# Mixers' output projection: four results side by side per input block, and high halves of its weights made on ScalarE

## The chip, the cores and the metric

The kernel runs on one core of a Trainium2 chip. The metric is the device time of one execution in microseconds (us), and smaller is better. TensorE is called PE in the rows (PEld is its weight load), VectorE DVE, ScalarE ACT, GpSimd POOL and SyncE SP.

## What is computed

The reference runs two blocks of a model over 256 tokens of 1024 channels, everything in float32. The first block has two layers. Each layer adds to the running state `h`, in this order: half of a gated feed-forward network, a "mixer", an attention to a memory of 256 rows, and half of a second feed-forward network. The change is in the mixer alone:

```python
p = u @ w_mix_in[l]
p_conv, p_hg, p_rw = jnp.split(p, (CONV_PROJ, CONV_PROJ + HG_PROJ), axis=-1)
y = jnp.concatenate([short_conv_mixer(p_conv, ...), hgrn2_mixer(p_hg, ...), rwkv7_mixer(p_rw, ...)], axis=-1)
h = h + y @ w_mix_out[l]
h = h + memory_cross_attention(rmsnorm(h, xattn_norm[l]), rmsnorm(mem, mem_norm[l]), ...)
```

`rwkv7_mixer` ends with a group norm over each head (mean and variance over 64 channels), a gain and an offset per channel, a bonus term and a gate; that gives the last 384 of the 1024 channels of `y`. `w_mix_out` is 1024 by 1024. The second block (attention over a context, a mixture of experts) follows and is not touched.

## The kernel before, in words

**Numbers in two halves.** A float32 product at the accuracy wanted is made from three products of a faster format: each operand is split into a high half (a cast, "hi") and a low half (the original minus the high half, "lo"), and `mm3` issues hi·hi, hi·lo and lo·hi into one PSUM bank. One block of 128 by 128 weights against 256 tokens is thus three matmuls (line 368, in `mm`).

**The weights come as a stream.** `Stream` (called `W`) holds all weights in the order of use, cut into chunks of 32 blocks (128 partitions by 4096 columns, 2 MB). SyncE loads chunk after chunk into three slots (L2103), and waits before each until TensorE has released the chunk that lay there. `split(c)` makes the two halves of chunk `c`, both on VectorE: a cast (L130) and a subtraction (L131). `blocks` hands out blocks in order. At the first block of chunk `c` it also queues `split(c + 1)`, so a chunk is split one chunk ahead; `prepare` queues the first split by hand. `toks` are the points of VectorE's queue that a matmul on the chunk waits for; each stands for eight blocks where a chunk was split in pieces.

**The queues.** Every engine takes its instructions in the order in which the program queued them, which is the order in which the Python code runs. On VectorE, ScalarE and GpSimd each instruction also waits for the one before it (`Queue`, chain true). There is no planner: an instruction that waits holds up all that are queued behind it on its engine. `barrier()` gives tokens for all that has been queued so far.

**PSUM.** `Banks` hands out the eight PSUM banks in turn; a matmul into a bank waits until the bank's last reader is done. During the mixer only banks 0 to 4 are in turn; before the output projection the turn is widened to all eight (`B.banks = psb`).

**The end of a mixer.** The order of the code, and so of the queues, is this. At the end of `rwkv` (call c the chunk with the first half of `w_mix_out`): the group norm's reductions on VectorE (L1135, L1139), a square root on ScalarE (L416 through `power`), the scaling by it on VectorE, and six transposes on TensorE (L397) into two banks, which are the last two of the five in turn. Then `W.prepare` queues `split(c)`. After it, for each of three groups of 128 channels, come four VectorE instructions (L405, L400: gain and offset, bonus, gate). Back in `mixer`: `Halves.make` splits `Y(5)` to `Y(7)` on VectorE (L388 the cast, L400 the subtraction); those of `Y(0)` to `Y(4)` were made before. `memory_squares` has GpSimd load the memory rows (L60, 1 MB), and queues on ScalarE eight squares of them (L416), which wait for that load. Then `linear` makes the eight results of the projection (m = 0 to 7), each from eight blocks (k = 0 to 7, one per 128 channels of `y`): 192 matmuls, two chunks, c and c + 1. For each result `evac2` adds it to `X(m)` (VectorE, L400) and calls `nxt.add`: the halves of the next norm's input on VectorE (L404, L408) and a square on ScalarE (L416). These halves are the operand of the next product, the attention's query (`xattn_wq`), whose first result needs all eight. Behind its first result stands `norms`, 32 matmul rows on TensorE for two root mean squares, and the chain on VectorE that hangs on them.

The order on ScalarE's queue around the projection is: the square root of the group norm, the eight squares of the memory rows, then one square for each result. On VectorE it is: `split(c)`, the twelve of the group norm's end, the halves of Y(5) to Y(7), `split(c + 1)`, the evacuations of m = 0 to 3 (three instructions each), `split(c + 2)`, the evacuations of m = 4 to 7, `split(c + 3)`.

Of the kernel before, what the change touches and what calls it, by code (L numbers as in the profile page):

```python
# [7 lines left out]
F32 = mybir.dt.float32  # L8
U32 = mybir.dt.uint32
F32R = mybir.dt.float32r  # L10
ALU = mybir.AluOpType
# [5 lines left out]
NHI = 2  # L17
D = 1024
KT = 8
# [89 lines left out]
class Stream:  # L109
# [3 lines left out]
    def __init__(self, ring, ring_r, hiring_r, sems, pe, dve, idle):  # L113
        self.ring, self.ring_r, self.hiring_r, self.pe, self.dve, self.idle = ring, ring_r, hiring_r, pe, dve, idle
        self.arrivals = [Arrival(s) for s in sems]
        self.specs, self.released, self.breaks, self.ahead, self.plain = [], {}, {}, {}, False

    def arrived(self, c):
        return (self.arrivals[c % NSLOT], 16 * (c // NSLOT + 1))

    def split(self, c, *after):

        n = CH * 128
        raw = self.ring[:, n * (c % NSLOT):n * (c % NSLOT) + n]
        lo = self.ring_r[:, n * (c % NSLOT):n * (c % NSLOT) + n]
        hi = self.hiring_r[:, n * (c % NHI):n * (c % NHI) + n]
        toks = []
        for a, b in ((0, 1024), (1024, 2048), (2048, 4096)) if c == 0 else ((0, 4096),):
            h, r, w = hi[:, a:b], raw[:, a:b], lo[:, a:b]
            self.dve(lambda e, h=h, r=r: e.tensor_copy(h, r), self.arrived(c), self.released.get(c - NHI), after)  # L130
            toks.append(self.dve(lambda e, h=h, r=r, w=w: e.tensor_tensor(w, r, h.bitcast(F32), ALU.subtract)))  # L131
        self.ahead[c] = (toks, len(self.dve.ops))

    def cancel(self, c):
# [138 lines left out]
def build(nc, x_t, mem_t, ctx_t, params, consts, na_bias, wexp, xd, yd, out, stop):  # L273
    es = ExitStack()
    with es:
# [36 lines left out]
        DVE = Queue("dve", True)  # L312
        ACTQ = Queue("act", True)
# [43 lines left out]
        def barrier():  # L357

            toks = [(q, q.n) for q in (DVE, ACTQ, POOL) if q.n]
            if PE.ops:  # L360
                toks.append(PE.mark())
            return toks
# [7 lines left out]
        def mm3(ps, a, b, start, stop, *after, inc=False):  # L370

            (ah, al), (bh, bl) = a, b
            mm(ps, ah, bh, start, False, after)
            mm(ps, ah, bl, False, False)
            return mm(ps, al, bh, False, stop, inc=inc)

        def as_r(ap):
            return arena_r[:, ap.offset:ap.offset + ap.shape[1]]
# [20 lines left out]
        def tt(q, out_, a, b, op, *after, **kw):  # L399
            return q(lambda e: e.tensor_tensor(out_, a, b, op), *after, **kw)  # L400
# [17 lines left out]
        def cp(q, out_, a, *after, **kw):  # L418
            if q is ACTQ:
                return q(lambda e: e.copy(out_, a), *after, **kw)  # L420
            return q(lambda e: e.tensor_copy(out_, a), *after, **kw)  # L421

        B = Banks(psb)

        def linear(key, r0, c0, nm, xs, evac, *after, kt=KT, n=256, between=None):

            toks = []
            for m in range(nm):
                ps, w = B.take()
                for k in range(kt):  # L430
                    wb, a = W.blocks(key, r0 + 128 * k, c0 + 128 * m)
                    t = mm3(ps[:, 0:n], wb, xs.at(k, 0, n), k == 0, k == kt - 1, w, a, after, xs.tok[k], inc=k == kt - 1)
                if m == 0 and between is not None:
                    between()
                tok = evac(m, ps, t)
                B.leave(ps, tok)
                toks.append(tok)
            return toks
# [179 lines left out]
        def mixer(l, pre, nxt):  # L618
            uh = pre.h
            Pr = Reg(8192, 29 * 256)  # L620
            P = lambda j, n=1: Pr.v(256 * j, 256 * n)
            Yr = Reg(8192 + 7424, 2048)
            Y = lambda j, n=1: Yr.v(256 * j, 256 * n)
            wk = 8192 + 7424 + 2048

            def evac(m, ps, t):
                return pre.scale(P(m), ps[:, 0:256], t)

            pt = linear(("w_mix_in", l), 0, 0, 29, uh, evac, between=pre.finish)
            W.mode(True)  # L630
            W2, wa = W.blocks(("w2a2", l), 0, 0, 3)
            G2, wa2 = W.blocks(("rwkv_g2", l), 0, 0, 3)
            wa = [wa, wa2]
            W.align(CH)
            wsm = Reg(6400, 768).v()
            tw2 = cp(POOL, wsm[:, 0:384], W2, wa, pt)
            tw2 = cp(POOL, wsm[:, 384:768], G2, wa)
            W2, G2, wa = wsm[:, 0:384], wsm[:, 384:768], [tw2]
            f = barrier()
            mm(MF[0:1, 0:1], con("col"), con("col"), True, True, f, wa)  # L640
            FILL.start(modulation(l, f))
            spare = ring[:, NSLOT * CH * 128:(NSLOT + NHI) * CH * 128]

            ha = hgrn(l, P, Y, wk, f)
            upto(ha, "logs")
            Z = Reg(6144, 520, spare)
            z = Z.t(260)
            t = DVE(lambda e: e.memset(Z.v(0, 520), 0.0), f)
            t = tt(DVE, z[:, :, 2:258], P(2, 2).rearrange("p (k w) -> p k w", w=256), P(4, 2).rearrange("p (k w) -> p k w", w=256), ALU.mult)
            T = Reg(6144 + 520, 512, spare)  # L650
            for j in range(2):
                tj = T.v(256 * j, 256)
                ts(DVE, tj, z[:, j, 0:256], par("conv_w", l, j), par("conv_b", l, j), ALU.mult, ALU.add)
                stt(tj, z[:, j, 1:257], par("conv_w", l, 2 + j), tj, ALU.mult, ALU.add)
                stt(tj, z[:, j, 2:258], par("conv_w", l, 4 + j), tj, ALU.mult, ALU.add)
                tconv = tt(DVE, Y(j), tj, P(j), ALU.mult)
            rb = rwkv(l, P, Y, Yr, wk, W2, G2, wa, spare, [f, tconv])
            FILL.step(4)
            upto(rb, "mixed")
            FILL.step(4)  # L660
            upto(ha, "scanned")
            upto(rb, "gates")
            FILL.step(6)
            upto(ha, "gates")
            upto(rb, "scanned")
            FILL.step(6)
            upto(ha, "turned")
            upto(rb, "keys")
            FILL.step(6)
            upto(rb, "bonus")  # L670
            upto(ha, "level")
            upto(rb, "hats")
            FILL.step(4)
            upto(ha, "level")
            upto(rb, "turned")
            FILL.step(4)
            for g in range(3):
                upto(rb, "first")
                upto(ha, "level")
                FILL.step(1)  # L680
            for i in range(18):
                upto(rb, "inverse")
                upto(ha, "level")
                FILL.step(0.5)
            upto(ha, "end")
            YH = Reg(22528, 2048)
            yh = Halves(Y, lambda k: YH.v(256 * k, 256))
            got_a = PE.mark()
            for k in range(5):
                yh.make(k, got_a)  # L690
            upto(rb, "end")
            f = barrier()
            B.banks = psb
            for k in range(5, KT):
                yh.make(k, f)

            mem = memory_squares(l, f)

            def evac2(m, ps, t):
                t = tt(DVE, X(m), ps[:, 0:256], X(m), ALU.add, t)  # L700
                nxt.add(m, t)
                return t

            linear(("w_mix_out", l), 0, 0, KT, yh, evac2, f)
            return mem

        def transpose_tiles(srcs, dst, q, *after):
# [193 lines left out]
                else:  # L901
                    yield "level"

        def rwkv(l, P, Y, Yr, wk, W2, G2, wa, spare, f):
            A, LW = Reg(2048, 768), Reg(2048 + 768, 768)
            E, G = Reg(8192, 768), Reg(8192 + 768, 768)
            KK, BON = Reg(Yr.base + 1280, 768), Reg(wk, 768)
# [15 lines left out]
            for j in range(3):  # L923
                ps, w = B.take()
# [3 lines left out]
                ps, w = B.take()  # L928
# [214 lines left out]
            bk = []  # L1143
            for b in range(2):
                ps, w = B.take()
                for j in range(3):
                    tk = tr(ps[:, 128 * j:128 * j + 128], YT.v(384 * b + 128 * j, 128), w, t, inc=j == 2)
                bk.append((ps, tk))
            W.prepare(got_y)
            for j in range(3):  # L1150
                for b, (ps, tk) in enumerate(bk):
                    s = slice(256 * j + 128 * b, 256 * j + 128 * b + 128)
                    ts(DVE, Y(5, 3)[:, s], ps[:, 128 * j:128 * j + 128], par("ln_w", l, j), par("ln_b", l, j), ALU.mult, ALU.add,
                       tk)
                tt(DVE, Y(5 + j), Y(5 + j), BON.v(256 * j, 256), ALU.add)
                tt(DVE, Y(5 + j), Y(5 + j), G.v(256 * j, 256), ALU.mult)
            for ps, tk in bk:
                B.leave(ps, (DVE, DVE.n))

# [1098 lines left out]
```

How the kernel before makes its waits and increments, by code:

```python
    def play(self, eng, a=0, b=None):  # L64
        seen = {}
        for waits, fn, inc in self.ops[a:b]:
            for q, v in waits:
                if seen.get(q.sem, 0) < v:
                    eng.wait_ge(q.sem, v)
                    seen[q.sem] = v
            ins = fn(eng)
            if inc:
                ins.then_inc(self.sem, 1)
# [1660 lines left out]
            def more(eng):  # L1734
                for q, v in flat(enter):
                    eng.wait_ge(q.sem, v)
                nested(SECTIONS[l][1:], [p[None] for p in parts[1:]])(eng)
# [238 lines left out]
            def ready(eng, toks):  # L1976
                for q, v in toks:
                    eng.wait_ge(q.sem, v)
# [108 lines left out]
        @block.sync  # L2087
        def _(sp):
            for dst, src, sem in LOADS[0:2]:
                sp.dma_start(dst, src).then_inc(sem.sem, 16)
            wait = 0
            for c in range(nchunk):
                if c in W.breaks:
                    ready, fn = W.breaks[c]
                    fn(sp)
                    for q, v in flat(ready):
                        sp.wait_ge(q.sem, v)
                if c >= NSLOT and W.released.get(c - NSLOT, (0, 0))[1] > wait:
                    wait = W.released[c - NSLOT][1]
                    sp.wait_ge(PE.sem, wait)
# [12 lines left out]
        @block.scalar  # L2114
        def _(eng):
            ACTQ.play(eng)
            for q, v in end:
                eng.wait_ge(q.sem, v)
            if stop < 9:
                eng.dma_start(out, Xr.v(0, 2048)).then_inc(A_out.sem, 16)
            else:
```

## Time and profile before

| what | value |
|---|---|
| median of three runs | 3903.55 us (3900.97 to 3910.81) |
| the profiled execution's own time | 3900.22 us |
| its span in the trace | 3898.2 us |
| mean granted TensorE clock | 0.941 |
| output projection of layer 0 (chunk c prepared to last result taken) | 525.0 to 565.3 us |
| the same in layer 1 | 1406.3 to 1446.3 us |

The span is the time from the first to the last instruction in the trace; the time of the execution is 2.0 us longer. All times in the rows are from the span's start. A row of the timeline is one instruction or a run of equal ones: its start, its length, the engine, the line, and in brackets how long the engine had been idle before it and what ended that.

### The profile page before, as it was taken

To read this page: it belongs to the slowest core of one execution; us is meant where nothing else is said; L and a number is where in the kernel's file an instruction comes from. 1 tells how busy PE (TensorE), PEld (TensorE's weight loads), DVE (VectorE), ACT (ScalarE), POOL (GpSimd) and SP (SyncE) were. 2 spreads that over 40 slices of the span, in tenths; PEclk is the share of its full clock that TensorE was granted. 3 is DMA by queue.
4 is the path that set the end of the run, shared out by engine and by line. 5 is a ranking of instruction groups with operands and counts; after the bars stand their busy time and mean duration, and the time that the engine had idled before them with its cause. 6 is when DMAs were issued, how large, how long until landed. Compare 5 with 4: busy or idle time off the path is not lost. (4 is left out here: it accounts for less than half of the span.)

```text
span 3898.2 us, 51672 instructions
## 1 busy us (share of the span) xinstructions
PE 3482.2 (89%) x20728; PEld 2834.7 (73%) x20728; DVE 2802.1 (72%) x3212; ACT 1174.9 (30%) x1555; POOL 448.2 (11%) x463
## 2 busy tenths in 40 slices
PE   8996878999996879998788999999559879999995
PEld 8993778999993778997555667767348656776774
DVE  8866687888876677886757777777264677777774
ACT  1003101100003101111323556556220245655652
POOL 0000200000000200101011212212011011221220
PEclk9997889999996889999999999999779999999998
DMA  6557023454556023551025999999433159999993
GB/s 238 184 185 280 1 83 126 172 193 173 195 190 259 5 76 130 184 189 71 22 72 191 367 367 360 363 358 370 174 130 119 55 189 336 337 345 338 335 342 130
DMA packets 118928, 802.66 MB, mean 206 GB/s; under 512 B 33808, under 2 KB 34832, under 8 KB 48272
## 3 DMA queue, kind: packets, MB, share of 16 engines
q1 hardware_dynamic: 77040, 714.17, 49.5%
q0 software_dynamic: 40592, 83.99, 6.0%
q8 instruction: 166, 2.72, 0.3%
q10 hardware_dynamic: 1040, 1.05, 0.1%
q14 instruction: 90, 0.74, 0.1%
HBM read 812.18 MB, written 71.83 MB: 227 GB/s over the span
## 5 line engine op out<-in xcount | busy, mean ns | idle before, releaser
L368 PE MATMUL ps<-arena_r,ring_r 128*128 128x256 f32 (+1 forms) x10224 | 1306.8, 289 | 87.6 <-POOL arena_r L400 30.0
L368 PEld LDWEIGHTS ps<-arena_r,ring_r 128*128 128x128 f32 x10224 | 1267.0, 190 | 124.3 <-POOL arena_r L400 35.1
L1864 PE MATMUL ps<-ring_r,arena_r 128*128 128x512 f32 x1880 | 554.2, 398 | 6.3 <-DVE arena_r L1880 6.3
L416 ACT ACTIVATE arena<-arena 128x256 f32<-128x256 f32 (+3 forms) x293 | 141.9, 484 | 1271.4 <-DVE arena L400 782.6
L131 DVE TENSOR_TENSOR ring_r<-ring,ring_r 128x4096 fp32r<-128x4096 f32 (+2 forms) x117 | 509.7, 4357 | 4.0
L1864 PE MATMUL ps<-ring,arena 128*128 128x512 f32 x1032 | 464.1, 592 | 1.6 <-DVE arena L1916 1.6
L1861 DVE TENSOR_TENSOR ring_r<-ring,arena_hi 128x2048 fp32r<-128x2048 f32 x152 | 348.4, 2292 | 97.7 <-ACT arena_hi L1860 89.1
L1864 PEld LDWEIGHTS ps<-ring_r,arena_r 128*128 128x128 f32 x1880 | 351.4, 189 | 81.3 <-DVE arena_r L1880 7.1
L1864 PE MATMUL ps<-arena_hi,arena_r 128*128 128x512 f32 x1216 | 401.2, 397 | 0.0
L368 PE MATMUL ps<-arena 128*128 128x128 f32 (+5 forms) x1728 | 261.7, 337 | 107.3 <-DMA arena<-yd_dram 42.5
L130 DVE CAST ring_r<-ring 128x4096 fp32r<-128x4096 f32 (+2 forms) x117 | 290.9, 2487 | 72.6 <-PE ps L368 60.4
L1864 PEld LDWEIGHTS ps<-ring,arena 128*128 128x128 f32 x1032 | 195.4, 190 | 198.0 <-issue 185.2
L368 PEld LDWEIGHTS ps<-arena 128*128 128x128 f32 (+1 forms) x1728 | 204.7, 216 | 157.9 <-ACT arena L420 52.2
L1861 DVE TENSOR_TENSOR ring_r<-ring,ring_r 128x2048 fp32r<-128x2048 f32 x106 | 242.9, 2292 | 73.3 <-ACT ring_r L1860 67.8
L1860 ACT CAST arena_hi<-ring 128x2048 fp32r<-128x2048 f32 x152 | 290.1, 1908 | 13.5 <-ACT arena_r L1879 0.4
L1864 PEld LDWEIGHTS ps<-arena_hi,arena_r 128*128 128x128 f32 x1216 | 229.2, 188 | 48.8
L1880 DVE TENSOR_TENSOR arena_r<-ps,arena_r 128x512 fp32r<-128x512 f32 x258 | 178.4, 692 | 97.2 <-ACT arena_r L1879 82.8
L1945 POOL DMA_INDIRECT yd_dram<-arena,small x129 | 129.8, 1006 | 1014.0 <-ACT arena_r L1879 930.6
L1860 ACT CAST ring_r<-ring 128x2048 fp32r<-128x2048 f32 x106 | 202.6, 1912 | 35.1 <-PE ps L368 18.5
L1930 ACT COPY arena<-ps 128x512 f32<-128x512 f32 x129 | 75.5, 585 | 397.2 <-PE ps L1864 397.2
L400 POOL TENSOR_TENSOR arena_r<-arena,arena_r 128x256 fp32r<-128x256 f32 (+1 forms) x104 | 84.7, 814 | 958.2 <-DVE arena_r L388 958.2
L421 DVE COPY arena<-ps 128x128 f32<-128x128 f32 (+3 forms) x172 | 68.7, 400 | 154.6 <-PE ps L368 141.9
(192 smaller groups left out, 3337.5 us busy)
## 6 DMA issues: line engine op xcount, KB each, us to landing
ring<-wexp_dram SPq DMA_DIRECT2D x387, 1024.0 KB, 8.1
ring<-stream_dram SPq DMA_DIRECT2D x145, 2048.0 KB, 7.7
arena<-yd_dram POOLq DMA_DIRECT2D x12, 2048.0 KB, 10.3
xd_dram<-arena POOLq DMA_DIRECT2D x6, 512.0 KB, 10.0
consts_sb<-consts_dram SPq DMA_DIRECT2D x1, 2241.5 KB, 15.8
arena<-xd_dram,small POOLq DMA_INDIRECT x129, 10.3
yd_dram<-arena,small POOLq DMA_INDIRECT x129, 8.2
arena<-mem_dram POOLq DMA_DIRECT2D x2, 1024.0 KB, 5.2
```

The lines of the kernel that those rows point to most:

```text
L130: self.dve(lambda e, h=h, r=r: e.tensor_copy(h, r), self.arrived(c), self.released.get(c - NHI), after)
L131: toks.append(self.dve(lambda e, h=h, r=r, w=w: e.tensor_tensor(w, r, h.bitcast(F32), ALU.subtract)))
L368: return PE(lambda e: e.matmul(ps, lhsT=lhsT, rhs=rhs, start=start, stop=stop, skip_group_check=True), *after, inc=inc)
L400: return q(lambda e: e.tensor_tensor(out_, a, b, op), *after, **kw)
L416: return ACTQ(lambda e: e.activation(out_, a, f, bias=bias, scale=scale), *after, **kw)
L421: return q(lambda e: e.tensor_copy(out_, a), *after, **kw)
L1860: t = Ac(lambda e: e.copy(hi, src), got(n), free)
L1861: split_tok[n] = Dv(lambda e: e.tensor_tensor(lo, src, hi.bitcast(F32), ALU.subtract), t)
L1864: return P(lambda e: e.matmul(out_, lhsT=x, rhs=y, start=st_, stop=sp_, skip_group_check=True), *after, inc=inc)
L1880: t2 = Dv(lambda e, hi=hi, lo=lo, ps=ps: e.tensor_tensor(lo, ps[:, :], hi.bitcast(F32), ALU.subtract), t2)
L1930: fn = (lambda e, dst=dst, ps=ps: e.copy(dst, ps[0:S, :])) if nn else \
L1945: Po.raw(lambda e: e.indirect_dma_start(out=yd, out_offset=bass.IndirectOffsetOnAxis(ap=pair_of[0:S, b0 + i:b0 + i + 1], axis=0), in_=YB[i ...
```

## The change

There are four edits. `linear` gets a parameter `wide`: with 4, results 0 to 3 are made together, the loop over the input blocks k outside and over the four results inside, and they are evacuated once all four are complete; results 4 to 7 go as before. `Stream` gets `by_act`: while it is set, `split` has ScalarE make the high half, and the subtraction on VectorE waits for it. A prepared chunk is then also split in three pieces (1024, 1024 and 2048 columns). `by_act` is set just ahead of `W.prepare` in `rwkv` and cleared behind the projection, so chunks c, c + 1 and c + 2 are split in that way. The high halves of Y(5) to Y(7) move to ScalarE, each behind its gate (`ytok`), and the barrier `f` is taken behind them; `linear` no longer waits for `f`.

```diff
--- before.py
+++ after.py
@@ -114,6 +114,7 @@
         self.ring, self.ring_r, self.hiring_r, self.pe, self.dve, self.idle = ring, ring_r, hiring_r, pe, dve, idle
         self.arrivals = [Arrival(s) for s in sems]
         self.specs, self.released, self.breaks, self.ahead, self.plain = [], {}, {}, {}, False
+        self.by_act = None
 
     def arrived(self, c):
         return (self.arrivals[c % NSLOT], 16 * (c // NSLOT + 1))
@@ -125,10 +126,14 @@
         lo = self.ring_r[:, n * (c % NSLOT):n * (c % NSLOT) + n]
         hi = self.hiring_r[:, n * (c % NHI):n * (c % NHI) + n]
         toks = []
-        for a, b in ((0, 1024), (1024, 2048), (2048, 4096)) if c == 0 else ((0, 4096),):
+        for a, b in ((0, 1024), (1024, 2048), (2048, 4096)) if c == 0 or self.by_act is not None and after else ((0, 4096),):
             h, r, w = hi[:, a:b], raw[:, a:b], lo[:, a:b]
-            self.dve(lambda e, h=h, r=r: e.tensor_copy(h, r), self.arrived(c), self.released.get(c - NHI), after)
-            toks.append(self.dve(lambda e, h=h, r=r, w=w: e.tensor_tensor(w, r, h.bitcast(F32), ALU.subtract)))
+            t = None
+            if self.by_act is not None:
+                t = self.by_act(lambda e, h=h, r=r: e.copy(h, r), self.arrived(c), self.released.get(c - NHI), after)
+            else:
+                self.dve(lambda e, h=h, r=r: e.tensor_copy(h, r), self.arrived(c), self.released.get(c - NHI), after)
+            toks.append(self.dve(lambda e, h=h, r=r, w=w: e.tensor_tensor(w, r, h.bitcast(F32), ALU.subtract), t))
         self.ahead[c] = (toks, len(self.dve.ops))
 
     def cancel(self, c):
@@ -422,10 +427,22 @@
 
         B = Banks(psb)
 
-        def linear(key, r0, c0, nm, xs, evac, *after, kt=KT, n=256, between=None):
+        def linear(key, r0, c0, nm, xs, evac, *after, kt=KT, n=256, between=None, wide=0):
 
             toks = []
-            for m in range(nm):
+            if wide:
+                bk = [B.take() for _ in range(wide)]
+                got = []
+                for k in range(kt):
+                    for m, (ps, w) in enumerate(bk):
+                        wb, a = W.blocks(key, r0 + 128 * k, c0 + 128 * m)
+                        t = mm3(ps[:, 0:n], wb, xs.at(k, 0, n), k == 0, k == kt - 1, w, a, after, xs.tok[k], inc=k == kt - 1)
+                        if k == kt - 1:
+                            got.append(t)
+                for m, (ps, w) in enumerate(bk):
+                    toks.append(evac(m, ps, got[m]))
+                    B.leave(ps, toks[m])
+            for m in range(wide, nm):
                 ps, w = B.take()
                 for k in range(kt):
                     wb, a = W.blocks(key, r0 + 128 * k, c0 + 128 * m)
@@ -654,7 +671,8 @@
                 stt(tj, z[:, j, 1:257], par("conv_w", l, 2 + j), tj, ALU.mult, ALU.add)
                 stt(tj, z[:, j, 2:258], par("conv_w", l, 4 + j), tj, ALU.mult, ALU.add)
                 tconv = tt(DVE, Y(j), tj, P(j), ALU.mult)
-            rb = rwkv(l, P, Y, Yr, wk, W2, G2, wa, spare, [f, tconv])
+            ytok = []
+            rb = rwkv(l, P, Y, Yr, wk, W2, G2, wa, spare, ytok, [f, tconv])
             FILL.step(4)
             upto(rb, "mixed")
             FILL.step(4)
@@ -689,11 +707,11 @@
             for k in range(5):
                 yh.make(k, got_a)
             upto(rb, "end")
-            f = barrier()
             B.banks = psb
             for k in range(5, KT):
-                yh.make(k, f)
-
+                t = cp(ACTQ, as_r(yh.hi(k)), Y(k), ytok[k - 5])
+                yh.tok[k] = tt(DVE, as_r(Y(k)), Y(k), as_r(yh.hi(k)).bitcast(F32), ALU.subtract, t)
+            f = barrier()
             mem = memory_squares(l, f)
 
             def evac2(m, ps, t):
@@ -701,7 +719,8 @@
                 nxt.add(m, t)
                 return t
 
-            linear(("w_mix_out", l), 0, 0, KT, yh, evac2, f)
+            linear(("w_mix_out", l), 0, 0, KT, yh, evac2, wide=4)
+            W.by_act = None
             return mem
 
         def transpose_tiles(srcs, dst, q, *after):
@@ -901,7 +920,7 @@
                 else:
                     yield "level"
 
-        def rwkv(l, P, Y, Yr, wk, W2, G2, wa, spare, f):
+        def rwkv(l, P, Y, Yr, wk, W2, G2, wa, spare, ytok, f):
             A, LW = Reg(2048, 768), Reg(2048 + 768, 768)
             E, G = Reg(8192, 768), Reg(8192 + 768, 768)
             KK, BON = Reg(Yr.base + 1280, 768), Reg(wk, 768)
@@ -1146,6 +1165,7 @@
                 for j in range(3):
                     tk = tr(ps[:, 128 * j:128 * j + 128], YT.v(384 * b + 128 * j, 128), w, t, inc=j == 2)
                 bk.append((ps, tk))
+            W.by_act = ACTQ
             W.prepare(got_y)
             for j in range(3):
                 for b, (ps, tk) in enumerate(bk):
@@ -1153,7 +1173,7 @@
                     ts(DVE, Y(5, 3)[:, s], ps[:, 128 * j:128 * j + 128], par("ln_w", l, j), par("ln_b", l, j), ALU.mult, ALU.add,
                        tk)
                 tt(DVE, Y(5 + j), Y(5 + j), BON.v(256 * j, 256), ALU.add)
-                tt(DVE, Y(5 + j), Y(5 + j), G.v(256 * j, 256), ALU.mult)
+                ytok.append(tt(DVE, Y(5 + j), Y(5 + j), G.v(256 * j, 256), ALU.mult))
             for ps, tk in bk:
                 B.leave(ps, (DVE, DVE.n))
```

## Rows read from the trace of the kernel before

**Rows 1.** The page's first part: busy time, share of the span, instructions.

```profile
PE 3482.2 (89%) x20728; PEld 2834.7 (73%) x20728; DVE 2802.1 (72%) x3212; ACT 1174.9 (30%) x1555; POOL 448.2 (11%) x463
```

**Rows 2.** Timeline, layer 0: group norm's end to the halves of Y(7).

```profile
523.73 0.21 ACT L416 ACTIVATE small<-small 128x12 f32<-128x12 f32 x1 [37.68 <-DVE small L443]
...
524.99 1.54 PE L397 MATMUL ps<-consts_sb,arena 128*128 128x128 f32 x6 [6.25 <-DVE arena L400]
525.04 2.29 DVE L130 CAST ring_r<-ring 128x4096 fp32r<-128x4096 f32 x1
...
527.37 4.43 DVE L131 TENSOR_TENSOR ring_r<-ring,ring_r 128x4096 fp32r<-128x4096 f32 x1
...
536.48 0.89 DVE L400 TENSOR_TENSOR arena<-arena 128x256 f32<-128x256 f32 x2
537.40 0.29 DVE L388 CAST arena_r<-arena 128x256 fp32r<-128x256 f32 x1
537.47 27.67 PE L368 MATMUL ps<-arena_r,ring_r 128*128 128x256 f32 x213 [10.94 <-DVE arena L400]
537.67 0.72 POOL L60 DMA_DIRECT2D arena<-mem_dram  x1 [57.42 <-DVE arena L400]
...
539.30 0.42 DVE L400 TENSOR_TENSOR arena_r<-arena,arena_r 128x256 fp32r<-128x256 f32 x1
```

**Rows 3.** The timeline on, to the attention's first product (layer 0).

```profile
539.83 2.29 DVE L130 CAST ring_r<-ring 128x4096 fp32r<-128x4096 f32 x1
...
543.03 3.58 ACT L416 ACTIVATE arena<-arena 128x256 f32<-128x256 f32 x8 [19.09 <-DMA arena<-mem_dram]
546.69 0.42 DVE L400 TENSOR_TENSOR arena<-ps,arena 128x256 f32<-128x256 f32 x1
...
548.13 0.42 DVE L400 TENSOR_TENSOR arena<-ps,arena 128x256 f32<-128x256 f32 x1
...
551.40 0.42 DVE L400 TENSOR_TENSOR arena<-ps,arena 128x256 f32<-128x256 f32 x1 [0.50 <-PE ps L368]
...
552.84 2.29 DVE L130 CAST ring_r<-ring 128x4096 fp32r<-128x4096 f32 x1
...
559.70 0.42 DVE L400 TENSOR_TENSOR arena<-ps,arena 128x256 f32<-128x256 f32 x1
...
565.40 0.63 PE L368 MATMUL ps<-arena_r,ring_r 128*128 128x256 f32 x3 [0.27 <-DVE arena_r L408]
565.45 2.29 DVE L130 CAST ring_r<-ring 128x4096 fp32r<-128x4096 f32 x1
...
565.87 7.07 PE L368 MATMUL ps<-arena,consts_sb 128*128 128x256 f32 x32
...
574.63 0.42 DVE L404 TENSOR_SCALAR mrow<-ps 128x256 f32<-128x256 f32 x1
```

**Rows 4.** Timeline, layer 1: squares of the memory rows, attention's first product.

```profile
1424.08 3.57 ACT L416 ACTIVATE arena<-arena 128x256 f32<-128x256 f32 x8 [19.24 <-DMA arena<-mem_dram]
...
1446.37 0.62 PE L368 MATMUL ps<-arena_r,ring_r 128*128 128x256 f32 x3 [0.26 <-DVE arena_r L408]
```

**Rows 5.** Groups by line and shape; after the bar busy us, then mean ns.

```profile
L1860 ACT CAST arena_hi<-ring 128x2048 fp32r<-128x2048 f32 x152 | 290.1, 1908 | 13.5 <-ACT arena_r L1879 0.4
...
L416 ACT ACTIVATE arena<-arena 128x256 f32<-128x256 f32 x202 | 84.5, 418 | 853.4 <-DVE arena L400 583.1 <-DVE arena L408 229.6 <-DMA arena<-mem_dram 38.3
L131 DVE TENSOR_TENSOR ring_r<-ring,ring_r 128x1024 fp32r<-128x1024 f32 x2 | 2.4, 1224 | 0.1
L131 DVE TENSOR_TENSOR ring_r<-ring,ring_r 128x2048 fp32r<-128x2048 f32 x1 | 2.3, 2293 | 0.0
```

**Rows 6.** Stretches: busy of PE, PEld, DVE, ACT, POOL; clock, DMA share, GB/s.

```profile
526.00:537.00 11.00, 0.53 (x3) 0.13 (x1) 10.39 (x14) 0.00 (x0) 0.00 (x0) 0.50 0.52 191
538.00:542.00 4.00, 4.00 (x21) 4.00 (x20) 3.76 (x6) 0.00 (x0) 0.39 (x1) 0.50 0.70 248
543.00:563.00 20.00, 20.00 (x172) 20.00 (x172) 18.30 (x22) 5.87 (x14) 0.00 (x0) 1.00 0.29 106
```

## The prediction, made before the change was run

> **What bounds the kernel now.** I read the page's busy times first [rows 1]: TensorE is busy for 89% of the span and VectorE for 72%, so over the whole kernel TensorE looks like the bound. That average doesn't hold here. I then read the timeline around the changed lines, in layer 0 [rows 2, 3] and layer 1 [rows 4]. From the group norm's end at 525.04 to 565.34 VectorE has one instruction behind the other, with one idle piece of 0.50 us at 551.40. TensorE waits for it instead: its last three matmuls of the attention's first result start at 565.40, released by VectorE (L408), the half of the state that the last evacuation makes. So the stage ends when VectorE's queue comes to the end of the eighth evacuation. I call that moment E: 565.34 in layer 0, some 1446.3 in layer 1. All that follows (VectorE goes on at 565.45, the norm's matmuls at 565.87) hangs on E. What the change is worth is the shift of E, twice.
>
> **Prices.** ScalarE's cast of 2048 columns takes 1.908 us and its activation of 256 columns 0.418 us [rows 5], which is 0.831 ns a column: an estimate of 1.06 us for 1024 columns and 3.61 us for 4096. Its upper bound is twice the row of 2048, 3.82; the lower bound is VectorE's own cast of that size, 2.29 [rows 2]. I take 3.61, since it comes from the same engine, the same kind of operation and half the size. A subtraction takes 1.22 us for 1024 columns, 2.29 for 2048 [rows 5] and 4.43 for 4096 [rows 2]. A handover between ScalarE and VectorE costs 0.04 us (the square root ends at 523.94, VectorE goes on at 523.98).
>
> **Part 1: the prepared chunk c.** The three casts are queued on ScalarE behind the square root, which ends at 523.94 [rows 2]. So they don't run beside the norm's reductions, only beside its last scaling: they end at 525.03, 526.1 and 528.06. The subtractions run from 525.07, 526.32 and, waiting for the third cast, 528.10; they end at 530.39, against 531.80 now (527.37 + 4.43). Gain 1.41 us. If ScalarE's casts cost nothing it would be 2.0.
>
> **Part 2: the halves of Y(5) to Y(7).** Now three pairs of cast and subtraction run from 537.40 to 539.72, and the next instruction starts at 539.83 [rows 2, 3]. With the casts on ScalarE beside the gates, VectorE is left three subtractions of 0.42 us and gaps, 1.38 us in all. They start at 535.96 (537.37 less 1.41) and VectorE is free at 537.4: 2.4 us earlier than now. The barrier is taken behind them, at 537.4, where it is taken now too (just ahead of the halves, at 537.37). So GpSimd still starts the load of the memory rows at about 537.67, and their landing still releases ScalarE's squares at 543.03.
>
> **Part 3: the wide loop on TensorE.** The first four results run k by k. A first matmul needs only the first piece of chunk c, so TensorE starts at 526.5, when the transposes end, and not at 537.47 [rows 2]. The transposes hold the last two of the five banks in turn, so the next four banks are free. At 1.2 GHz (clock 0.50) 4 us hold some 19 matmuls, 0.21 us each; at 2.4 GHz 20 us hold 170, 0.118 us each [rows 6]. The 60 matmuls of k = 0 to 4 take 12.8 us at the slow clock and some 9 if it rises on the way, as it does between 542 and 543 now. The last 36 wait for the halves of Y(5) to Y(7) and end at 540.8, or at 545 with the slow clock. Now the first 96 end at 551.4, where the fourth evacuation stops waiting [rows 3]. TensorE gains 6 to 10 us, but this buys nothing: next it needs chunk c + 1, and E was VectorE's.
>
> **Part 4: chunk c + 1, where the time is lost.** Its cast is queued when `linear` asks for the first block, behind `memory_squares`. Now it is on VectorE (539.83 to 542.12) and waits for nothing. After the change it is on ScalarE's queue behind eight squares that wait for the memory rows until 543.03 and end at 546.61 [rows 3]. The cast runs from 546.64 to 550.25, the subtraction from 550.30 to 554.73. Queued behind this subtraction on VectorE are the four evacuations, though their sums are complete; VectorE stands idle from 537.4 to 550.3. The first evacuation starts at 554.83, not 546.69: E is 8.1 us later so far.
>
> That an engine never passes a waiting instruction decides this. The row shows ScalarE idle for 19.09 us until the memory load lands. The Trainium skill (TensorE: Matmul & The Clock Gate, "Architectural detail: the array is 16× 32×32, not 1× 128×128") says that ScalarE and VectorE are strict first-in, first-out, while TensorE may pull weight loads ahead. By this rule the cast waits, as worked out here; if ScalarE could pull ahead as TensorE does, the sum would be that of the faster rival below.
>
> **Part 5: chunk c + 2.** Four evacuations at 1.44 us each (546.69 to 548.13) follow without the idle 0.50. The fourth's addition ends at 554.83 + 4.32 + 0.42 = 559.57, its square on ScalarE at 560.03. Only then comes the cast of chunk c + 2, to 563.67; the subtraction ends at 568.14, and the fifth evacuation starts at 568.24, against 559.70 now. So VectorE is spared 2.29 us of cast and idles over 3 us for it. TensorE has chunk c + 1 at 554.8; at the slow clock, to which it falls in the 14 us pause (it stood at 0.50 in the pause of now [rows 6]), the fifth result is done at 560 and the eighth before 569. None is late. The last four evacuations take 5.64 us as now: E = 573.9, **8.5 us later**.
>
> **Layer 1** has the same rows, with the squares ending at 1424.08 + 3.57 = 1427.65 [rows 4]. In layer 0 E comes 27.3 us behind that end (573.9 less 546.6); the same steps give E = 1454.9. Now TensorE is released at 1446.37, so E is 1446.3: **8.6 us later**.
>
> **The rest.** The stream's loads are released no later than they are needed: chunk c + 3 may load 10 us earlier. It starts when the memory rows are nearly through; a delay of these moves E by as much, 0 to 1 us a layer, and I take 0. Dropping the wait for `f` has no cost, its parts are waited for elsewhere.
>
> **Sum.** 8.5 + 8.6 = +17.1 us. The profiled execution took 3900.22 us (span 3898.2 and 2.0 around it), so 3917.3 is due for it. It lies 3.3 below the median, and the forecast is the median plus the shift: 3903.55 + 17.1 = **3920.7 us**. With ScalarE's cast at 3.82 it is 3921.5. A measurement of this kernel can tell about 0.3% from no change, which is 11.7 us.
>
> **The rivals.**
> - *The clock takes more.* After the change TensorE works in small pieces while the last evacuations run, and may meet the 32 matmul rows of the norms (7.07 us [rows 3]) at 1.2 GHz: 7 us more at most. The second of the norm's values is taken at 574.63, 1.7 us behind their end, so up to 5 us a layer could be added: up to 3930.7. The Trainium skill (TensorE: Matmul & The Clock Gate, "Why this matters for your kernels") warns of idle gaps between bursts of matmuls, since the clock falls back in them; the trace agrees (0.50 in the pause before the projection). Against the rival: VectorE's 6.7 us of splitting right behind E cover the first half of the slow rows, and the clock may be up again by then. Chance 0.15.
> - *The delay is absorbed in part, or the big cast is cheap.* At VectorE's 2.29 us a cast, each layer loses 5.9 and the result is 3915.4, the edge of what can be told; any wait behind E that had slack brings it to 3905 to 3915. Against it: VectorE has no idle row right behind E, and ScalarE's price lies on its own rows. Chance 0.12.
> - *Faster: the cast isn't held by the memory rows.* It decides whether the cast of chunk c + 1 can start at once, before 537.4; the rows would have to land, or the squares to be passed. Then its subtraction runs 537.4 to 541.8, the evacuations 541.9 to 547.6, chunk c + 2's cast ends at 550.8, its subtraction at 555.3 and E = 561.0: 4.3 us earlier a layer, 3894.9. If both casts were hidden, VectorE would be spared three casts of 2.29 and three of 0.29 less 0.3 for the pieces, 7.5 a layer: 3888.5. For it: VectorE is the bound here and loses work. Against it: the order of ScalarE's queue. Chance 0.06.
>
> **How the numbers follow.** My forecast has 0.67, its own range 3916 to 3926 (the casts' upper bound, the memory load, the spread of the runs). The clock's rival makes it 3930.7 at most; the range goes down to the absorbed case's upper half: 3911 to 3931. Slower by over 0.3% is forecast and clock, 0.82; within 0.3% 0.12; faster 0.06.
>
> **What the profile will show.** Right: two casts of 128x4096 on ScalarE in each layer, the first one right behind the eight squares, of about 3.6 us; VectorE idle some 13 us ahead of a subtraction of 4096 (in `split`) released by ScalarE; TensorE idle about 14 us between the halves of the projection; the first product of the attention held until about 574. Wrong: a cast of chunk c + 1 ahead of the squares, a first product before 566, or one much later than 575 with the evacuations waiting for TensorE.

## The result, and the profile after

The changed kernel takes 3926.16 us (median of 5 runs, 3922.27 to 3929.02) against 3900.97 us before (5 runs, 3898.96 to 3910.81). The ratio on record is 1.0056 with a 95% interval of 1.0043 to 1.0068: 21.8 us slower (0.0056 of 3901), between 16.8 and 26.5. It is not the quotient of the two medians, which is 1.0065 and lies inside the interval (25.2 us). All ratios below are those on record. The profiled execution took 3924.95 us, its span is 3923.0 us.

The page's busy line, to be laid beside [rows 1]: VectorE did 14.3 us less, ScalarE 24.8 us more, and the span grew by 24.8.

```profile
PE 3496.0 (89%) x20728; PEld 2842.7 (72%) x20728; DVE 2787.8 (71%) x3204; ACT 1199.7 (31%) x1571; POOL 444.4 (11%) x463
```

Next the timeline of layer 0 after, from the group norm's first reduction to the load of the memory rows, as [rows 2]. The lines of the file have moved: the reduction is L1154 (it was L1135), ScalarE's weight cast L133, VectorE's subtraction L136, evacuations L405, matmuls L373.

```profile
521.22 0.95 DVE L1154 TENSOR_REDUCE small<-arena 128x12 f32<-128x768 f32 x1
...
526.18 4.05 ACT L133 CAST ring_r<-ring 128x1024 fp32r<-128x1024 f32 x3
...
528.53 8.47 PE L373 MATMUL ps<-arena_r,ring_r 128*128 128x256 f32 x60
...
528.95 3.62 DVE L136 TENSOR_TENSOR ring_r<-ring,ring_r 128x1024 fp32r<-128x1024 f32 x2 [0.47 <-DVE ring_r L136]
...
538.26 1.48 DVE L405 TENSOR_TENSOR arena_r<-arena,arena_r 128x256 fp32r<-128x256 f32 x3
538.74 4.51 PE L373 MATMUL ps<-arena_r,ring_r 128*128 128x256 f32 x36 [1.74 <-DVE arena_r L405]
540.05 0.72 POOL L60 DMA_DIRECT2D arena<-mem_dram  x1 [57.66 <-DVE arena_r L405]
```

Up to here the change does what it was made to do. TensorE's 60 matmuls run during the norm's end, the first four results are complete at 543.25 (538.74 + 4.51), and VectorE is free at 539.74, 18.5 us behind the reduction and not 20.6. The timeline on, as [rows 3]:

```profile
545.55 3.55 ACT L421 ACTIVATE arena<-arena 128x256 f32<-128x256 f32 x8 [6.96 <-DMA arena<-mem_dram]
549.19 3.60 ACT L133 CAST ring_r<-ring 128x4096 fp32r<-128x4096 f32 x1
552.82 4.42 DVE L136 TENSOR_TENSOR ring_r<-ring,ring_r 128x4096 fp32r<-128x4096 f32 x1 [13.08 <-ACT ring_r L133]
557.30 15.58 PE L373 MATMUL ps<-arena_r,ring_r 128*128 128x256 f32 x111 [14.06 <-DVE ring_r L136]
557.35 0.42 DVE L405 TENSOR_TENSOR arena<-ps,arena 128x256 f32<-128x256 f32 x1
...
562.65 3.62 ACT L133 CAST ring_r<-ring 128x4096 fp32r<-128x4096 f32 x1
566.30 4.42 DVE L136 TENSOR_TENSOR ring_r<-ring,ring_r 128x4096 fp32r<-128x4096 f32 x1 [3.30 <-ACT ring_r L133]
570.83 0.42 DVE L405 TENSOR_TENSOR arena<-ps,arena 128x256 f32<-128x256 f32 x1
...
576.53 1.01 PE L373 MATMUL ps<-arena_r,ring_r 128*128 128x256 f32 x3 [0.70 <-DVE arena_r L413]
...
577.34 9.52 PE L373 MATMUL ps<-arena,consts_sb 128*128 128x256 f32 x32
...
586.89 0.42 DVE L409 TENSOR_SCALAR mrow<-ps 128x256 f32<-128x256 f32 x1 [1.24 <-PE ps L373]
```

Read it by the brackets. VectorE stands idle for 13.08 us, released by ScalarE's cast; that cast starts 0.09 us behind the end of the eight squares, and these were released by the load of the memory rows. TensorE idles for 14.06 us behind the subtraction. The second big cast makes VectorE wait 3.30 us more. In layer 1 the same two waits are 12.96 and 3.31 us.

The last two lines are a second loss. The 32 rows of the norms take 9.52 us and not 7.07, and VectorE waits 1.24 us for them, where before it didn't. The stretches of that piece show the clock (columns as in [rows 6]):

```profile
570.00:573.60 3.60, 2.88 (x23) 2.51 (x21) 3.25 (x7) 0.83 (x2) 0.00 (x0) 1.00 0.52 109
573.60:575.50 1.90, 1.03 (x6) 0.82 (x6) 1.62 (x4) 0.42 (x1) 0.00 (x0) 0.99 1.05 448
575.50:582.30 6.80, 6.10 (x17) 4.82 (x17) 6.59 (x5) 0.42 (x1) 0.00 (x0) 0.50 0.30 128
582.30:587.00 4.70, 4.70 (x24) 4.16 (x24) 3.32 (x4) 0.42 (x1) 0.00 (x0) 1.00 0.00 0
```

TensorE worked in pieces of three matmuls while it waited for the last evacuations, fell to 1.2 GHz (0.50) at 575.5 and was back at 2.4 GHz at 582.3.

**How the runs below are measured.** The span of one kernel varies by some us from run to run, also where nothing is changed: the group norm's first reduction, up to which all programs here are the same, starts between 516.7 and 521.2 us in the ten profiles. So the table gives distances from this reduction. Each kernel has one profile, so how well they repeat is seen only from its two layers: they agree within 0.5 us in every kernel. D ends at the start of the last three matmuls of the attention's first result (before 565.40 - 519.10 = 46.3). S ends at the first evacuation of that product, behind the norms: it holds what the change costs or brings up to that point. "Rows" is the time of the 32 matmul rows of the norms. The last column is the ratio on record with its interval, each against the runs of the kernel before that stood beside it.

| kernel | layer 0: reduction, last three, D | S | layer 1: reduction, last three, D | S | rows, layers 0 and 1 | time against before |
|---|---|---|---|---|---|---|
| before | 519.10, 565.40, 46.3 | 68.7 | 1399.99, 1446.37, 46.4 | 68.8 | 7.1, 7.1 | |
| after | 521.22, 576.53, 55.3 | 78.8 | 1412.32, 1467.49, 55.2 | 78.7 | 9.5, 9.5 | 1.0056 (1.0043 to 1.0068) |
| e1, squares behind | 519.71, 564.57, 44.9 | 68.6 | 1400.73, 1445.57, 44.8 | 68.4 | 9.7, 9.6 | 1.0008 (0.9999 to 1.0017) |
| e2, prepared chunk only | 519.79, 563.58, 43.8 | 66.2 | 1397.30, 1441.10, 43.8 | 66.2 | 8.6, 8.4 | 0.9985 (0.9975 to 0.9995) |
| e3, casts ahead | 519.75, 558.83, 39.1 | 61.5 | 1393.58, 1432.62, 39.0 | 61.4 | 7.1, 7.1 | 0.9969 (0.9957 to 0.9981) |
| e4, not wide | 518.27, 573.30, 55.0 | 78.5 | 1408.91, 1464.00, 55.1 | 78.6 | 9.4, 9.5 | 1.0053 (1.0037 to 1.0068) |
| e5, squares twice | 516.74, 575.68, 58.9 | 82.5 | 1411.48, 1469.98, 58.5 | 82.0 | 9.5, 9.5 | one run, 3925.26 us |
| e6, kept busy | 517.41, 572.87, 55.5 | 77.9 | 1407.91, 1462.92, 55.0 | 77.4 | 7.1, 7.1 | 1.0039 (1.0024 to 1.0055) |
| e7, ahead, not wide | 518.19, 561.99, 43.8 | 66.2 | 1395.40, 1439.20, 43.8 | 66.2 | 7.1, 7.1 | 0.9989 (0.9977 to 1.0001) |
| e8, wide alone | 517.72, 567.06, 49.3 | 71.7 | 1401.58, 1451.20, 49.6 | 72.0 | 8.8, 8.8 | 1.0013 (1.0001 to 1.0026) |

The kernel before ran beside e1 to e4 at 3903.93 us (22 runs) and beside e5 to e8 at 3901.45 us (25 runs). S grew by 10.1 us in layer 0 and 9.9 in layer 1 with the change: 20.0 of the 21.8 us measured.

### The profile page after: what moved, and what is told of

Same layout as the page of the kernel before. It is cut to its first block and busy times, and to the rows that moved or that the text cites. A ratio compares the mean times of both kernels' runs of the same rounds, so it can differ in the third digit from the quotient of the medians.

```text
span 3923.0 us, 51696 instructions
## 1 busy us (share of the span) xinstructions
PE 3496.0 (89%) x20728; PEld 2842.7 (72%) x20728; DVE 2787.8 (71%) x3204; ACT 1199.7 (31%) x1571; POOL 444.4 (11%) x463
## 3 DMA queue, kind: packets, MB, share of 16 engines
q10 hardware_dynamic: 1040, 1.05, 0.1%
## 5 line engine op out<-in xcount | busy, mean ns | idle before, releaser
L373 PE MATMUL ps<-arena_r,ring_r 128*128 128x256 f32 (+1 forms) x10224 | 1306.6, 289 | 97.3 <-DVE ring_r L136 47.9
L373 PEld LDWEIGHTS ps<-arena_r,ring_r 128*128 128x128 f32 x10224 | 1264.0, 191 | 136.4 <-DVE ring_r L136 44.6
L136 DVE TENSOR_TENSOR ring_r<-ring,ring_r 128x4096 fp32r<-128x4096 f32 (+2 forms) x121 | 510.3, 4218 | 38.0 <-ACT ring_r L133 33.5
L373 PE MATMUL ps<-arena 128*128 128x128 f32 (+5 forms) x1728 | 264.1, 339 | 107.1 <-DMA arena<-yd_dram 41.9
L135 DVE CAST ring_r<-ring 128x4096 fp32r<-128x4096 f32 (+2 forms) x111 | 277.6, 2501 | 70.9 <-PE ps L373 59.5
L373 PEld LDWEIGHTS ps<-arena 128*128 128x128 f32 (+1 forms) x1728 | 207.1, 218 | 157.6 <-ACT arena L425 52.2
L405 POOL TENSOR_TENSOR arena_r<-arena,arena_r 128x256 fp32r<-128x256 f32 (+1 forms) x104 | 84.7, 815 | 971.4 <-DVE arena_r L393 971.4
L426 DVE COPY arena<-ps 128x128 f32<-128x128 f32 (+3 forms) x172 | 68.7, 399 | 155.0 <-PE ps L373 142.2
## 6 DMA issues: line engine op xcount, KB each, us to landing
arena<-yd_dram POOLq DMA_DIRECT2D x12, 2048.0 KB, 10.2
arena<-xd_dram,small POOLq DMA_INDIRECT x129, 10.4
```

Source lines behind the costliest of these rows:

```text
L373: return PE(lambda e: e.matmul(ps, lhsT=lhsT, rhs=rhs, start=start, stop=stop, skip_group_check=True), *after, inc=inc)
```

## The experiments

**e1: is it the place in the queue, or ScalarE's slower cast?** The squares are queued behind the projection; nothing else changes.

```diff
-            return [(sqs.v(256 * k, 256), act(sqs.v(256 * k, 256), MEMr.v(256 * k, 256), ACT.Square, got, f))
+            return lambda: [(sqs.v(256 * k, 256), act(sqs.v(256 * k, 256), MEMr.v(256 * k, 256), ACT.Square, got, f))
                     for k in range(KT)]
...
-            return mem
+            return mem()
```

> The changed kernel with one edit: the eight squares of the memory rows are queued on ScalarE behind the output projection, not ahead of it; the load itself starts as before. D is the distance from the group norm's first reduction to the start of the last three matmuls of the attention's first result: 46.3 us in the kernel before, 55.3 after. Queue order (my theory): the cast of chunk c + 1 starts right behind the last cast of Y(7), 3.6 us long, so its subtraction starts some 4 us behind the barrier and not 13; everything up to D comes 10.6 us earlier than after, D = 44.7, and the time is that of the kernel before or a few us less, 3895 to 3902. Rival (ScalarE's slower cast is what costs, wherever it is queued): D stays above 50 and the time within 8 us of after.

D fell by 10.4 and 10.3 us, to 44.9 and 44.8: the place in the queue is what costs. The timeline of e1 shows the cast right behind that of Y(7), and a wait of 2.61 us in place of 13.08:

```profile
536.68 0.40 ACT L425 CAST arena_r<-arena 128x256 fp32r<-128x256 f32 x1 [1.41 <-DVE arena L405]
537.20 3.62 ACT L133 CAST ring_r<-ring 128x4096 fp32r<-128x4096 f32 x1
...
540.85 4.43 DVE L136 TENSOR_TENSOR ring_r<-ring,ring_r 128x4096 fp32r<-128x4096 f32 x1 [2.61 <-ACT ring_r L133]
...
550.68 3.62 ACT L133 CAST ring_r<-ring 128x4096 fp32r<-128x4096 f32 x1
554.34 4.43 DVE L136 TENSOR_TENSOR ring_r<-ring,ring_r 128x4096 fp32r<-128x4096 f32 x1 [3.31 <-ACT ring_r L133]
```

The time was over what I expected (3907.35 us against 3895 to 3902; ratio 1.0008): of the 1.5 us that D gains on the kernel before, the rows of the norms give back 1.2 to 1.4, being 9.7 and 9.6 us long at the fallen clock, so S is hardly better than before. And ScalarE's casts do cost something even so: VectorE's two remaining waits, 2.61 and 3.31 us, are for them. Beside e2, where VectorE makes these two casts itself, D is 1.1 us longer.

**e2: the big casts back on VectorE.** ScalarE casts the prepared chunk alone.

```diff
             W.prepare(got_y)
+            W.by_act = None
```

> The changed kernel, but ScalarE casts the prepared chunk c alone; chunks c + 1 and c + 2 are cast on VectorE as before the change. My theory: VectorE is never idle for long again; the gains of the prepared chunk and of Y(5) to Y(7) remain, 2.4 us, and the 0.5 us wait for TensorE goes: D = 43.8 against 46.3 before, time about 5 us below the kernel before, 3895 to 3899. Rival (the three pieces, the wide loop or the moved barrier cost something of their own): D above 46.3.

D is 43.8, as worked out, and the kernel is a little faster than before: ratio 0.9985 (0.9975 to 0.9995). The median, 3900.67 us beside 3903.93, is above the 3895 to 3899 that I expected. S lies 2.5 and 2.6 us below before. The rows of the norms took 8.6 and 8.4 us, but S less D is 22.4 us, as before: a fall of the clock of that size reaches nothing behind it. So the prepared chunk, the three pieces, the halves of Y(5) to Y(7) and the moved barrier are a small gain; the loss is in the other two chunks.

**e3: both casts hidden.** The casts are queued where ScalarE has nothing to do, and the squares go behind the projection as in e1.

```diff
+    def cast_high(self, c, *after):
+        n = CH * 128
+        h, r = self.hiring_r[:, n * (c % NHI):n * (c % NHI) + n], self.ring[:, n * (c % NSLOT):n * (c % NSLOT) + n]
+        self.high[c] = self.by_act(lambda e: e.copy(h, r), self.arrived(c), after)
...
             W.prepare(got_y)
+            W.cast_high(len(W.specs) // CH + 1, got_y)
...
+                W.cast_high(len(W.specs) // CH + 1, got[-1])
                 for m, (ps, w) in enumerate(bk):
                     toks.append(evac(m, ps, got[m]))
```

`split` takes the token of a cast that is already queued. The high halves have two slots (`NHI`), so the cast of chunk c + 2 overwrites those of chunk c; that is why it waits for the last matmul of the wide loop.

> The changed kernel with ScalarE's casts queued where they can run early: chunk c + 1 right behind the prepared one, chunk c + 2 right behind the wide loop and ahead of the evacuations, the squares of the memory rows behind the projection. My theory: both casts are hidden, VectorE is spared three casts of 2.29 us and three of 0.29; D = 39.1, 7.2 us a layer below the kernel before, time 3885 to 3890. Rival (VectorE gets nothing from it, since TensorE with 192 matmuls becomes the bound or ScalarE's and VectorE's accesses slow each other): D above 43, or subtractions of 4096 columns longer than 4.43 us.

D is 39.1 and 39.0, S is 7.2 and 7.3 us below before, and the time is 3890.88 us against 3903.93, just above the 3885 to 3890 that I expected: ratio 0.9969, some 12 us faster than before (0.0031 of 3904) and some 34 us faster than the change as it was made (0.9969 against 1.0056). The timeline of e3 (casts ahead are L123, subtractions L144) has no wait for ScalarE left:

```profile
538.31 4.43 DVE L144 TENSOR_TENSOR ring_r<-ring,ring_r 128x4096 fp32r<-128x4096 f32 x1
...
541.86 3.62 ACT L123 CAST ring_r<-ring 128x4096 fp32r<-128x4096 f32 x1 [4.74 <-PE ps L381]
...
542.79 13.78 PE L381 MATMUL ps<-arena_r,ring_r 128*128 128x256 f32 x114 [1.01 <-DVE ring_r L144]
...
548.60 4.42 DVE L144 TENSOR_TENSOR ring_r<-ring,ring_r 128x4096 fp32r<-128x4096 f32 x1
...
559.29 7.07 PE L381 MATMUL ps<-arena,consts_sb 128*128 128x256 f32 x32
```

**e4: the wide order undone.**

```diff
-            linear(("w_mix_out", l), 0, 0, KT, yh, evac2, wide=4)
+            linear(("w_mix_out", l), 0, 0, KT, yh, evac2)
```

> The changed kernel with the results of the projection made one after the other again (wide = 0), all else as after. My theory: TensorE is not the bound here, since its next chunk comes only at 36 us behind the reduction; D stays at 55.3 within 0.5 us and the time is that of after within 3 us. Rival (the late chunk comes from the wide order): D falls by several us.

D is 55.0 and 55.1, the time 3925.56 us (ratio 1.0053, beside 1.0056 with the wide order): the wide order neither caused the loss nor brought anything in this kernel. Now 81 matmuls wait for Y(5) and the first 96 end at about 548 (535.77 + 12.30), but chunk c + 1 comes only at 554.

**e5: more of the suspected wait.** Each square is issued twice.

```diff
-                    for k in range(KT)]
+                    for k in list(range(KT)) * 2][KT:]
```

> The changed kernel with each of the eight squares of the memory rows issued twice (same result, 3.6 us more on ScalarE). My theory: the cast of chunk c + 1 stands behind them, and VectorE idles for it, so D grows by the whole 3.6 us, to 58.9 in both layers, and VectorE's idle time ahead of the subtraction from 13.1 to 16.7 us. Rival (something else released the subtraction, the stream's load for one): D stays at 55.3.

D rose by 3.6 us in layer 0 and 3.3 in layer 1, and VectorE's idle time ahead of the subtraction became 16.69 us. From e5's timeline:

```profile
541.10 7.13 ACT L421 ACTIVATE arena<-arena 128x256 f32<-128x256 f32 x16 [6.99 <-DMA arena<-mem_dram]
548.32 3.60 ACT L133 CAST ring_r<-ring 128x4096 fp32r<-128x4096 f32 x1
551.96 4.43 DVE L136 TENSOR_TENSOR ring_r<-ring,ring_r 128x4096 fp32r<-128x4096 f32 x1 [16.69 <-ACT ring_r L133]
```

What stands ahead of the cast on ScalarE comes through one for one: the squares took 3.58 us more (7.13 less 3.55). In layer 1, where I had expected 58.9, they also began 0.27 us earlier behind the reduction than in after (1435.40 and 1436.51), and D is 58.5. The time of this single run, 3925.26 us, doesn't show it: its reduction started 4.5 us earlier than that of after, a difference from a part which is the same in both.

**e6: the clock.** Extra matmuls fill TensorE's three short waits in the attention's first result.

```diff
+                    if m == 0 and k in warm:
+                        nb = B.banks[B.i % len(B.banks)]
+                        for _ in range(8):
+                            mm(nb[:, 0:n], wb[0], xs.at(k, 0, n)[0], True, True, B.left.get(id(nb), []))
...
-                        between=norms)
+                        between=norms, warm=(4, 5, 6))
```

> The changed kernel with eight extra matmuls behind each of the blocks k = 4, 5, 6 of the attention's first result, into the next bank in turn, whose content the next first matmul overwrites: they fill TensorE's three waits for the last evacuations. The theory of the clock: the 32 matmul rows of the norms then take 7.1 us and not 9.5, the step from D to the second reciprocal falls from 10.8 to 9.7 us as before the change, and D itself stays at 55.3; the time is about 2 us below after, 3921 to 3926 against before at 3903. Rival (the rows are slow for another reason, such as the load of the stream beside them): they stay at 9.5.

The rows fell to 7.07 us and the step from D to the second reciprocal from 10.8 us (587.35 - 576.53) to 9.7 (582.55 - 572.87), with D unchanged. From e6's timeline; the row at 582.09 has no wait in its brackets any more:

```profile
573.33 7.07 PE L373 MATMUL ps<-arena,consts_sb 128*128 128x256 f32 x32
...
582.09 0.43 DVE L409 TENSOR_SCALAR mrow<-ps 128x256 f32<-128x256 f32 x1
```

So the second loss is the clock's, and it is about 1 us a layer: S less D is 22.4 us again, as before, where after has 23.5. The time, 3920.65 us, is just below the 3921 to 3926 that I expected; its ratio, 1.0039, has an interval that overlaps with that of after, so the times alone wouldn't show it. The load of the stream is out as a cause also by the traces: before the change the rows ran in 7.07 us with the DMA engines half busy (share 0.50 from 565.8 to 573.0), after it in 9.52 us with them nearly idle (0.03 from 577.3 to 587.0).

**e7: what the wide order is worth when the casts are hidden.** e3, with the results one after the other and chunk c + 2's cast behind the fourth.

```diff
-            linear(("w_mix_out", l), 0, 0, KT, yh, evac2, wide=4)
+            linear(("w_mix_out", l), 0, 0, KT, yh, evac2, high_at=3)
...
+                if m == high_at:
+                    W.cast_high(len(W.specs) // CH + 1, t)
```

> The kernel with the casts ahead (e3), but the results of the projection one after the other; chunk c + 2's cast is queued behind the fourth result's matmuls and ahead of its evacuation. My theory: now TensorE decides, since of chunk c only the first result's first five blocks can run before the halves of Y(5): the fourth result is done near 550 and not 542, and D is 43.1 against 39.1, the time 8 us above that of e3. Rival (the wide order is worth nothing here either): D = 39.1 within 0.5.

D is 43.8, 4.7 us above e3 (I had expected 43.1), and the time 0.9989 of before, with an interval that includes no change; e3 has 0.9969. Three waits of VectorE that e3 doesn't have make up the difference: two for TensorE, 1.17 us ahead of the third evacuation and 1.49 ahead of the fourth, and one of 2.37 for the cast of chunk c + 2, which could start only when TensorE was done with the fourth result:

```profile
535.71 26.07 PE L381 MATMUL ps<-arena_r,ring_r 128*128 128x256 f32 x198 [7.24 <-DVE arena_r L413]
...
548.04 0.42 DVE L413 TENSOR_TENSOR arena<-ps,arena 128x256 f32<-128x256 f32 x1 [1.49 <-PE ps L381]
548.09 3.63 ACT L123 CAST ring_r<-ring 128x4096 fp32r<-128x4096 f32 x1 [1.99 <-PE ps L381]
...
551.75 4.42 DVE L144 TENSOR_TENSOR ring_r<-ring,ring_r 128x4096 fp32r<-128x4096 f32 x1 [2.37 <-ACT ring_r L123]
```

**e8: the wide order alone, on the kernel before.**

```diff
-            linear(("w_mix_out", l), 0, 0, KT, yh, evac2, f)
+            linear(("w_mix_out", l), 0, 0, KT, yh, evac2, f, wide=4)
```

> The kernel before with the wide loop alone, everything else as before. My theory: the first four results are complete only when all 96 matmuls are, near 551.2 on the clock of the trace before; the first evacuation waits for that from 546.7 on, and since VectorE has nothing else queued ahead, all behind it moves by 4 us: D = 50.3, time 8 us above the kernel before. Rival (the wide order is neutral on its own): D = 46.3.

D grew by 3.0 and 3.2 us, where I had expected 4, and the time by 0.13% (0.01 to 0.26%; the medians lie 9.3 us apart). The direction is as expected, the size in D smaller: the 96 matmuls ended 31.0 us behind the reduction (548.74 - 517.72), where I had worked out 32.1 (551.2 - 519.10).

```profile
548.74 0.42 DVE L400 TENSOR_TENSOR arena<-ps,arena 128x256 f32<-128x256 f32 x1 [3.52 <-PE ps L368]
```

So in D the same edit costs 3 us a layer alone, is neutral in the change, and brings 4.7 us beside hidden casts.

## Why the prediction was right

The way, the mechanism and its place were right; the sum was 17.1 us, and 21.8 (16.8 to 26.5) were measured. Against the forecast of 3920.7 us stand 3926.16: that is inside the stated range of 3911 to 3931, but 0.16 us above the forecast's own 3916 to 3926, in the part that the range has from the clock's rival. The median from which the forecast started, 3903.55 us of three runs, is 2.6 above that of the five runs on record, so the forecast time came out nearer by luck of its base: from 3900.97 the same sum gives 3918.1. Point by point, as distances from the first reduction (519.10 before, 521.22 after):

- **Part 1.** The prepared chunk's last subtraction was to end at 11.3 us (530.39); it ended at 11.35 (528.95 + 3.62). The casts stand behind the square root, as worked out.
- **Part 2.** VectorE was to be free at 18.3; it was at 18.5.
- **Part 3.** The first 96 matmuls were to end at 21.7, or 26 with the slow clock; they ended at 22.0. That this buys nothing is shown by e4.
- **Part 4.** The subtraction of chunk c + 1 was to start at 31.2; it started at 31.6. The cast took 3.60 us where 3.61 was estimated. The 0.4 us are the memory rows': their squares began 24.3 us behind the reduction (545.55), not 23.9 (543.03), which the prediction had put at 0 out of 0 to 1. More than half of it is that GpSimd issued the load 18.8 us behind the reduction (540.05) and not 18.6 (537.67). e1 and e5 show that the cast's place behind the squares is the cause.
- **Part 5.** The fifth evacuation was to start at 49.1; it started at 49.6, behind a wait of 3.30 us. The shift of D came to 9.0 and 8.8 us against 8.5 and 8.6.
- **The clock's rival** was not an alternative but an addition, and it was oversized: up to 5 us a layer, against 1.1. The term of the sum that was missing is this one, and e6 takes it away. What the prediction said against the rival held: VectorE was splitting beside the slow rows (6.72 us from 576.58), and the clock was up again at 582.3. The rival rested on these small pieces, and so far it was right; beside it stood the warning of idle gaps between bursts, and those ahead of the fall were 0.78 and 0.82 us long.
- **The faster rival** failed where the prediction put its condition, the order of ScalarE's queue. With the squares alone out of the way (e1) the cast started 17.5 us behind the reduction (537.20), a microsecond before VectorE was free, but ended at 21.1: the rival's 4.3 us took it for done by then, and D was 1.4 and 1.5 us below before. With the casts queued ahead as well (e3) the larger gain appears: 7.2 and 7.3 us in D, where the prediction gave 7.5 for casts that are wholly hidden. No run shows whether ScalarE could pass a waiting instruction by itself: the program makes each of its instructions wait for the one before (`Queue`, chain true), which is enough to hold the cast.
- **Absorption** is out: the distance from the reduction of layer 0 to that of layer 1 grew from 880.89 to 891.10 us, by 10.2 us, and S had lost 10.1 in layer 0.

The sum of S over both layers, 20.0 us, lies within the measured interval. Of the 24.8 us between the two profiled spans, the rest lies outside the changed part: 2.1 us ahead of the first reduction, and 2.6 behind the end of S in layer 1. No run assigns these; they are of the size by which the first stretch varies between profiles of equal code.

## What to carry to other kernels

Before work is moved to an idle engine, write down that engine's queue at the place and look for an instruction that waits on a transfer: a cast of 3.6 us behind it cost 9 us, since it blocked VectorE's queue as well. The idle share of an engine (ScalarE 30%) tells nothing about when it is free. Here the slower engine paid where its casts were queued ahead of the need (e3), and brought next to nothing where they were queued when the need arose (e1). And measure a small change by distances between marks inside the trace: the two layers of a profile agreed within 0.5 us, while whole runs of the kernel before lay over 20 us apart (3893.38 to 3916.72).

## What was not expected of the hardware

- In e2 GpSimd's issue of the memory load took 2.21 and 2.20 us in the two layers, and not 0.72 and 0.60 as before, and the squares began 7.1 us behind its start (538.62 to 545.68), against 5.4 before (537.67 to 543.03). It is the one kernel in which VectorE's cast of 4096 columns runs just then:

```profile
538.42 2.29 DVE L135 CAST ring_r<-ring 128x4096 fp32r<-128x4096 f32 x1
538.62 2.21 POOL L60 DMA_DIRECT2D arena<-mem_dram  x1 [57.67 <-DVE arena_r L405]
```

  The issue ends 0.12 us behind the cast's end (540.71). The Trainium skill (SBUF — State Buffer, "SBUF: two separate sides", and in it "A bandwidth-pool intuition that's wrong (but worth ruling out)") says that GpSimd can't write its descriptors while VectorE runs an fp32 copy from SBUF to SBUF, and that it is blocked until about 115 ns behind the copy's end; the trace agrees. A cast on ScalarE doesn't do this: in e1 one of 4096 columns runs beside the issue (537.20 to 540.82), which took 0.72 us.
- TensorE lost its clock without a long pause. In after it waited for 0.70 to 0.82 us ahead of each of the last three pieces of three matmuls; it was busy for 2.88 of 3.60 us, then for 1.03 of 1.90 us (573.6 to 575.5), and went to 1.2 GHz (0.50). With the gaps filled (e6) it stayed at 2.4 GHz (1.00). Three such pieces stand ahead of the rows in e1, e2 and e8 too, and the clock fell in each. In e3 there are two, and it didn't: TensorE was busy for 1.05 of 2.70 us (556.5 to 559.2) at a clock of 1.00, and the rows took 7.07 us.
